# Query up-projection of the latent heads in five products, its weights split later, and the latent copies placed one by one

## The reference

```python
MLA_NOPE, MLA_ROPE, MLA_V = 64, 32, 64
MLA_Q_RANK, MLA_KV_RANK = 192, 128

def mla_q(zcq, g, w_uq, tabs):
    q = (rms_norm(zcq, g) @ w_uq).reshape(B, L, MLA_HEADS, MLA_NOPE + MLA_ROPE)
    q_nope, q_pe = jnp.split(q, [MLA_NOPE], axis=-1)
    if tabs is not None:
        q_pe = axial_rope(q_pe, tabs)
    return jnp.concatenate([q_nope, q_pe], axis=-1)

def mla_kv(zckv, zkr, g, w_ukv, tabs):
    kv = (rms_norm(zckv, g) @ w_ukv).reshape(B, L, MLA_HEADS, MLA_NOPE + MLA_V)
    k_nope, v = jnp.split(kv, [MLA_NOPE], axis=-1)
    ...
# per layer: adaLN -> one input projection -> o_a, o_b, o_m -> gates -> h @ w_out -> post-norm residual
o_m = block_attention(ql_m, jnp.concatenate([kc_m, kl_m], 1), jnp.concatenate([vc_m, vl_m], 1), MLA_SCALE)
```

## Time and profile before

| what | value |
|---|---|
| three runs | 953.35, 954.07, 954.11 us |
| profiled execution, its own time | 948.69 us |
| its span, first to last instruction | 946.6 us |
| busy: PE, DVE, POOL, ACT | 906.8, 560.1, 509.3, 429.5 us |
| mean granted clock of TensorE | 0.995 |
| instructions | 13414 |

### The profile page before, as it was taken

The page is one execution under the profiler, slowest core; times in us unless marked ns, Lnnn a source line. Parts: engine busy times, 40 slices in busy tenths (PEclk is TensorE's granted clock), DMA queues, the critical chain, the costliest instruction groups (busy, mean ns, idle before and its releaser), DMA issues.

```text
span 946.6 us, 13414 instructions
## 1 busy us (share of the span) xinstructions
PE 906.8 (96%) x4647; PEld 643.3 (68%) x4647; DVE 560.1 (59%) x903; ACT 429.5 (45%) x879; POOL 509.3 (54%) x433
## 2 busy tenths in 40 slices
PE   4999999999999999999999899999998999999996
PEld 3787767889745565665678789888984445555684
DVE  6569043513678679963318838567247758983347
ACT  5332121413566466655334853235335646655432
POOL 3246233324677645565547438455439876666572
PEclk9999999999999999999999999999999999999998
DMA  9968561314524200010343212323343221020252
GB/s 319 293 231 273 210 247 50 84 34 105 132 52 101 51 18 18 18 68 1 145 171 110 103 32 76 81 76 84 80 116 77 70 49 26 18 76 1 91 177 89
DMA packets 51753, 95.83 MB, mean 101 GB/s; under 512 B 9508, under 2 KB 24720, under 8 KB 50664
## 3 DMA queue, kind: packets, MB, share of 16 engines
q1 hardware_dynamic: 51688, 94.99, 33.1%
HBM read 71.32 MB, written 4.21 MB: 80 GB/s over the span
## 4 chain that ended last, share of the span: by engine, by line
PE 80%; DVE 7%; ACT 6%; POOL 2%; issue 2%; DMA 1%; SPq 1%; POOLq 0%; ACTq 0%; DVEq 0%
PE banks L998 14%; PE banks L1000 13%; PE banks L999 13%; PE banks L1293 13%; PE banks L1315 11%; PE banks L1238 4%; ACT area_z L1852 2%; PE banks L1009 2%; PE banks L1334 2%; PE banks L1267 1%; DVE negmax L2245 1%; PE banks L1327 1%; ACT late_bias L1829 1%; DMA w_raw<-in_w_in_dram 1%; DVE area_b L2422 1%
## 5 line engine op out<-in xcount | busy, mean ns | idle before, releaser
L1961 POOL TENSOR_TENSOR w_split<-w_raw,w_split 128x512 fp32r<-128x512 f32 (+4 forms) x122 | 146.8, 1212 | 216.2 <-ACT w_split L1570 216.2
L998 PE MATMUL banks<-w_split,area_a 128*128 128x512 f32 (+3 forms) x612 | 232.2, 379 | 6.3 <-POOL w_split L1961 3.2
L1000 PE MATMUL banks<-w_split,area_a 128*128 128x512 f32 (+3 forms) x612 | 224.9, 367 | 0.0
L999 PE MATMUL banks<-w_split,area_a 128*128 128x512 f32 (+3 forms) x612 | 224.3, 367 | 0.0
L2245 DVE TENSOR_REDUCE negmax<-banks 128x1 f32<-128x768 f32 x160 | 148.0, 951 | 79.7 <-PE banks L1238 55.9
L1570 ACT ACTIVATE w_split<-w_raw 128x512 fp32r<-128x512 f32 (+4 forms) x122 | 69.0, 580 | 195.8 <-PE banks L1000 183.5
L1688 ACT ACTIVATE area_z<-banks 128x512 f32<-128x512 f32 x196 | 108.2, 599 | 77.8 <-PE banks L1293 74.6
L998 PEld LDWEIGHTS banks<-w_split,area_a 128*128 128x128 f32 x612 | 115.5, 189 | 39.0 <-issue 19.1
L1293 PE MATMUL banks<-area_a 97*128 97x512 f32 (+4 forms) x448 | 127.8, 401 | 4.2 <-ACT area_z L1688 3.1
L1000 PEld LDWEIGHTS banks<-w_split,area_a 128*128 128x128 f32 x612 | 115.4, 188 | 16.5
L999 PEld LDWEIGHTS banks<-w_split,area_a 128*128 128x128 f32 x612 | 115.7, 189 | 12.8
(11 more groups left out here) (234 smaller groups left out, 1454.1 us busy)
## 6 DMA issues: line engine op xcount, KB each, us to landing
w_raw<-in_w_in_dram SPq DMA_DIRECT2D x32, 512.0 KB, 3.6
area_g<-in_w_ada_dram SPq DMA_DIRECT2D x13, 1024.0 KB, 5.3
area_g<-in_w_ada_dram SPq DMA_DIRECT2D x16, 512.0 KB, 5.5
w_raw<-in_w_out_dram SPq DMA_DIRECT2D x16, 512.0 KB, 4.8
area_a<-parts SPq DMA_DIRECT2D x72, 96.0 KB, 2.2
area_a<-parts SPq DMA_DIRECT2D x30, 192.0 KB, 3.6
area_b<-in_x_dram SPq DMA_DIRECT2D x8, 512.0 KB, 6.7
w_raw<-in_w_in_dram SPq DMA_DIRECT2D x8, 352.0 KB, 5.3
```

Source lines behind the costliest of these rows:

```text
L998: nc.tensor.matmul(dst, a[0], b[0], start=first, stop=False)
L999: nc.tensor.matmul(dst, a[0], b[1], start=False, stop=False)
L1000: return nc.tensor.matmul(dst, a[1], b[0], start=False, stop=last)
L1961: op = nc.gpsimd.tensor_tensor(lo, raw, hi.bitcast(F32), ALU.subtract)
```

## The change

The change has five parts, all in the attention or just ahead of it.

1. The rank of 192 is cut in 128 + 64 rows (`UQ = 128`). Of the second block the high part lies in rows 0 to 63 and the low part in rows 64 to 127 of the same tile; its weight slice of 64 rows is loaded twice, into rows 0 to 63 and 64 to 127 of its slot, with a second DMA. One product against the stacked block then does what two did, and a group of columns takes five products instead of six (three for block 0, two for block 1; the term low*low comes with them).
2. ACT: the copy of a unit's queries (`mla_high`) and that of its keys (`mla_high_keys`) are separate calls. The first unit's stand on either side of `exponent(p, 1)`, the second unit's on either side of `exponent(p, 3)`, where before both were ahead of `exponent(p, 2)`.
3. DVE: `mla_low` of both units stands behind `reduce_max(p+2, 1)`. Before, the first stood ahead of `reduce_max(p+1, 7)` and the second ahead of `reduce_max(p+2, 1)`.
4. PE: `max_tile` of a latent pair waits for the high parts instead of the low parts; the first score of the pair waits for the low parts of its second unit.
5. POOL splits slice 0 of `w_uq` in loop 0 and slice 1 in loop 3 (ACT's order of these stays). At the start of layer 0, POOL's split of the second slice of input weights waits until DVE has split the first rows of the normalized tokens (`h_ready`).

```diff
@@ constants, and the loading of the weights (SP) @@
-UQ = 96
+UQ = 128
...
                 elif kind == "uq":
-                    sp.dma_start(slot[0:UQ].rearrange("p a n -> p (a n)")[:, 0:576],
-                                 w_uq[L, a * UQ:(a + 1) * UQ, :]).then_inc(done, 16)
+                    flat = slot.rearrange("p a n -> p (a n)")[:, 0:576]
+                    if a == 0:
+                        sp.dma_start(flat, w_uq[L, 0:UQ, :]).then_inc(done, 16)
+                    else:
+                        rest = RANK_Q - UQ
+                        sp.dma_start(flat[0:rest], w_uq[L, UQ:RANK_Q, :]).then_inc(done, 16)
+                        sp.dma_start(flat[rest:2 * rest], w_uq[L, UQ:RANK_Q, :]).then_inc(done, 16)
...
@@ PE: mla_head, max_tile, scores @@
                     if what == "q":
-                        for j in range(2):
-                            mm = three(dst, [uq[:, i, j, h * P:(h + 1) * P] for i in range(2)],
-                                       [cmp_t[0:UQ, 2 * i + j, tokens(g)] for i in range(2)], j == 0, j == 1)
+                        w = [[uq[:, i, j, h * P:(h + 1) * P] for i in range(2)] for j in range(2)]
+                        three(dst, w[0], [cmp_t[:, 2 * i, tokens(g)] for i in range(2)], True, False)
+                        both = cmp_t[:, 1, tokens(g)]
+                        nc.tensor.matmul(dst, w[1][0], both, start=False, stop=False)
+                        mm = nc.tensor.matmul(dst, w[1][1], both, start=False, stop=True)
...
                     if family(u) == "mla":
-                        pe.wait_ge(mla_lo, N_MLA[L, u])
+                        pe.wait_ge(mla_hi, N_MLA[L, u])
...
                 if step == 0:
                     pe.wait_ge(mrow_in, 32 * (PN[L, p] + 1))
+                    if pair_family(p) == "mla":
+                        pe.wait_ge(mla_lo, N_MLA[L, 2 * p + 1])
@@ ACT: compressed_hi, mla_high, attend @@
-                r0, r1, hi = [(0, 96, 0), (0, 96, 1), (0, 128, 4), (64, 96, 6)][j]
+                r0, r1, hi = [(0, 128, 0), (0, 64, 1), (0, 128, 4), (64, 96, 6)][j]
...
-                f = operands(u)
-                copy(f[0][0:96, qcols(L)], qk_t[0:96, 2 * (m % 2), qcols(L)])
-                copy(f[2][0:64, :], qk_t[0:64, 2 * (m % 2) + 1, :]).then_inc(mla_hi, 1)
+                copy(operands(u)[0][0:96, qcols(L)], qk_t[0:96, 2 * (m % 2), qcols(L)])
+
+            def mla_high_keys(L, u):
+                m = N_MLA[L, u]
+                copy(operands(u)[2][0:64, :], qk_t[0:64, 2 * (m % 2) + 1, :]).then_inc(mla_hi, 1)
...
                     exponent(L, p, 1)
+                    if head_pair(p + 2):
+                        mla_high_keys(L, 2 * p + 4)
                     if context:
                         copy_context(L, p - 1)
                     else:
                         copy_latents(L, p - 1)
+                    exponent(L, p, 2)
+                    copy_denominators(L, p - 1)
                     if head_pair(p + 2):
                         mla_high(L, 2 * p + 5)
-                    exponent(L, p, 2)
-                    copy_denominators(L, p - 1)
                     exponent(L, p, 3)
                     copy_maxrow(L, p + 1)
+                    if head_pair(p + 2):
+                        mla_high_keys(L, 2 * p + 5)
                     if head_pair(p + 3):
                         mla_copy(L, 2 * p + 6)
@@ POOL @@
                     for s in chunks[0][:NW]:
+                        if s[3] == 1:
+                            pool.wait_ge(h_ready, N_H[0, 0, 0])
                         split_w(s)
...
-                    if p == 0:
-                        for j in range(2):
-                            split_w(("uq", L, j, 0))
+                    if p in (0, 3):
+                        split_w(("uq", L, int(p > 0), 0))
@@ DVE: compressed_lo, attend @@
-                    r0, r1, hi, lo = [(0, 96, 0, 2), (0, 96, 1, 3), (0, 128, 4, 5), (64, 96, 6, 7)][j]
+                    r0, r1, hi, lo = [(0, 128, 0, 2), (0, 64, 1, 1), (0, 128, 4, 5), (64, 96, 6, 7)][j]
+                    at = 64 if j == 1 else r0
...
-                    if head_pair(p + 2):
-                        mla_low(L, 2 * p + 4)
                     if not packed(p + 1):
                         reduce_max(L, p + 1, 7)
                     reduce_max(L, p + 1, 8)
...
-                    if head_pair(p + 2):
-                        mla_low(L, 2 * p + 5)
                     if not packed(p + 2):
                         reduce_max(L, p + 2, 1)
+                    if head_pair(p + 2):
+                        mla_low(L, 2 * p + 4)
+                        mla_low(L, 2 * p + 5)
                     if p == 2:
                         split_last(L)
                     reduce_max(L, p + 2, 2)
```

More of the change, by code:

```diff
@@ L291 @@
 for _n, _p in enumerate(PIECES):
-    _landed[_n % NRAW] += 16 * (len(CHUNKS[_p[2]]) if _p[0] == "in" else 1)
+    _landed[_n % NRAW] += 16 * (len(CHUNKS[_p[2]]) if _p[0] == "in" else 2 if _p[0] == "uq" and _p[2] else 1)
     RAW_VALUE[_p] = _landed[_n % NRAW]
@@ L496, in hybrid_layers @@
         ada_w = area_g[:].rearrange("p t d -> p (t d)").rearrange("p (s n) -> p s n", s=NADA)
-        uq = w_split[0:UQ].rearrange("p a b n -> p (a b n)").rearrange("p (s j n) -> p s j n", s=2, j=2)
+        uq = w_split[:].rearrange("p a b n -> p (a b n)").rearrange("p (s j n) -> p s j n", s=2, j=2)
         c_rows = scr[0:32, 1, 0:P]
@@ L965, in w_views @@
                 return [(src[:, z], hi[:, z], lo[:, z]) for z in range(2)]
-            src = flat[0:UQ, 0:576].rearrange("p (h n) -> p h n", h=6)
+            src = flat[:, 0:576].rearrange("p (h n) -> p h n", h=6)
             hi, lo = (uq[:, i, a, :].rearrange("p (h n) -> p h n", h=6) for i in range(2))
@@ L1141, in turn_compressed @@
                 _, L, j, g = use
-                a, b = [(0, 96), (96, 192), (192, 320), (256, 352)][j]
+                a, b = [(0, UQ), (UQ, RANK_Q), (192, 320), (256, 352)][j]
                 freed(pe, use)
@@ L2223, in compressed_lo @@
                     dve.wait_ge(hi_ready, N_HI[use])
-                    r0, r1, hi, lo = [(0, 96, 0, 2), (0, 96, 1, 3), (0, 128, 4, 5), (64, 96, 6, 7)][j]
-                    nc.vector.tensor_tensor(cmp_t[r0:r1, lo, tokens(g)], bank(use)[r0:r1, 0:len(GROUPS[g]) * P],
+                    r0, r1, hi, lo = [(0, 128, 0, 2), (0, 64, 1, 1), (0, 128, 4, 5), (64, 96, 6, 7)][j]
+                    at = 64 if j == 1 else r0
+                    nc.vector.tensor_tensor(cmp_t[at:at + r1 - r0, lo, tokens(g)], bank(use)[r0:r1, 0:len(GROUPS[g]) * P],
                                             cmp_t[r0:r1, hi, tokens(g)].bitcast(F32), ALU.subtract).then_inc(free_dve, 1)
```

## The result

The changed kernel takes 956.91 us, the median of six runs (956.46 to 958.39), against 953.7 us for the kernel before: a ratio of 1.0042, with a 95% interval of 1.0029 to 1.0056. It is slower, where 951.9 and faster was forecast.

The account below looks back on a forecast made before the run. PE, busy 96% of the span, was taken as the bound, with DVE near its limit in loops 5 and 6. Terms -1.2 + 0.1 + 0.2 - 1.1 - 0.2 = -2.2 us gave a 951.9 median, range 947.2 to 956.0.

Parts of the forecast that it names:

- Loop 7: Four subtractions ahead of reduce_max(9, 2) on DVE would cost 0 to +0.8 us a layer, +0.2 for both layers.
- Loops 5 and 6: One PE wait goes, another comes: +0.4 and -0.2 us in layer 0, +0.2 and -0.3 in layer 1, +0.1 together.
- The new wait: In loop 5, score (5,4)'s second product waits for ACT's copy to area_b, held by DVE's low part, until 357.6 to 359.6.
- The forecast's shift of 1.16: PE's first up-projection of loop 5 in layer 0 would come 1.16 us earlier, at 354.6 instead of 355.76.
- The 0.49: The maximum's wait of 0.49 us at 360.07 in loop 5 would go, since max_tile waits for the copy.
- The five products: 18 products fewer, 3.7 us; only pair 7's in loop 4 count separately, -1.2; the other 2.5 lie in loops 5 and 6.
- The late split: POOL's split of slice 1 moved to loop 3 removes a transfer wait in loop 1 of layer 1, -1.1 us.
- The second DMA of the slice: The extra load of 64 rows goes out among loads that land long before loop 4; no cost given.
- The start: POOL's second weight split waits for DVE's first rows, ready some 0.4 us earlier: -0.5 to +0.2, taken as -0.2.
- Rival C: Contended ends in loops 5 and 6 of both layers, two waits over 2 us bring half clock: +3.9, 958.0 us; chance 0.14.
- contended ends: High ends for loops 5 and 6, where subtractions take 1.92 to 2.04 us beside POOL: +3.0 over the four loops.
- The base: Profiled execution of the kernel before, 948.69 us, with the runs' median taken as 5.4 above it.

Follow-up runs that it names:

- e9: Changed kernel without POOL's wait at the start, first unit's copies and low part in their old places in loop 7 only: 952.1 us, ratio 0.9997.
- e10: Changed kernel without POOL's wait at the start, first unit's copies and low part in their old places in loops 5 and 6 only: 953.29 us, ratio 1.0011.
- e3: Changed kernel with the first unit's low part back in its old place on DVE, ACT's order as changed: 952.92 us, ratio 1.0008.
- e2: Changed kernel without POOL's wait for h_ready at the start: 955.41 us, ratio 1.0037.
- e12: e5 with PE's maxima waiting for the copies and a latent pair's first score for the low parts: 947.29 us, ratio 0.9943.
- e5: Kernel before with the five products and POOL's split of slice 1 in loop 3, old ACT and DVE orders: 947.85 us, ratio 0.9966.
- e4: Kernel before with the five products alone, all orders and waits as before: 949.6 us, ratio 0.9973.
- e6: Changed kernel without POOL's wait at the start, ACT's copies in the order before, DVE's low parts as changed: 963.2 us, ratio 1.0116.
- e11: Changed kernel with only the second unit's copies and low part moved, POOL's wait at the start kept: 947.59 us, ratio 0.995.
- e8: Changed kernel without POOL's wait at the start, only the second unit's copies and low part moved: 948.13 us, ratio 0.9957.

## Why the prediction was wrong

**Loop 7, the step that failed.** It was costed at "0 to +0.8 in a layer", +0.2 for both together, on the ground that "nothing of it shows where PE has products of its own for 2 us". Measured without a fall of the clock, loop 7 grew by 2.4 to 2.5 us in layer 0 (25.4, 25.5 against 23.0) and 1.7 in layer 1, +4.2 instead of +0.2. I had set the added work against PE's 2 us of products and had not asked when DVE gets to it: from 408.52 it works without a pause to 417.7, two of the four subtractions stand beside POOL's sums (2.06 and 2.02), and the reduction that PE wants is four subtractions, 5.7 us, behind the one before it. The forecast took such contended rows for loops 5 and 6 only. e9 shows the size (0.0040 of the time), e10 that the loss is there without loops 5 and 6, and e3, where only DVE's first low part went back, that DVE's row makes it: loop 7 is back at 23.0 and 19.7.

**Loops 5 and 6, right in mechanism.** The new wait is where the forecast put it, released by what it named. Up to loop 4 the changed kernel's profile runs 1.8 us behind the first one, by the fall of the clock at its start. Taken back by that, PE's second score product, forecast between 357.6 and 359.6, came at 358.7 (360.50 - 1.8), in the middle: one of the two subtractions was contended (2.03), the other hardly (1.07). The forecast's shift of 1.16 was more than its own terms give, 1.03 + 0.74 - 0.8 = 0.97; the first up-projection came at 356.57 - 1.8 = 354.8, where 354.6 was said. The loops as a whole (products included) changed by +0.2 and +0.1 in layer 0 and by +0.7 (e2, without a fall) and -0.4 in layer 1, +0.6 together, against +0.1. The 0.49 taken off because `max_tile` waits for the copy has no ground in that edit: in e12, which has it, the wait is 0.84, as it is 0.83 without it in e5.

**The five products, sized too small.** Loop 4 and its like in layer 1 gave 1.3 us, where 1.2 was said. But loops 5 and 6 gave 1.1 more (e4), though I had written that DVE near its limit makes a saved product worth little there. The time is 2.6 us lower by the ratio with the five products alone (1.2 to 4.0 by the interval), 3.1 by the medians.

**The late split, right**: -1.0 in loop 1 of layer 1 (forecast -1.1). That POOL works 55 to 60% of loop 3 was misread: in the kernel before it is busy for 13.47 of 19.22 us there in layer 0, 70%, and more in layer 1. No loss shows from the added split. **The second DMA of the slice**, costed at nothing, may not be: in every kernel with five products "between" is 0.5 to 1.2 us longer, and PE waits there for the transfer of ones_r, 0.4 to 1.1 us, where neither profile of before has such a wait. I did not run the doubled load by itself, so the cause stays open. **The start**: forecast -0.2, not measurable.

**The clock.** Rival C had the mechanism but asked for contended ends in all four loops and put two falls at the copy's waits, at 0.14. What came had one fall behind a wait of each kind, and the main loss from loop 7. By the runs' own records, (1 - clock) x span is 9.9 us for the changed kernel and 8.2 for the 26 runs of before, 5.0 for e5 and 12.2 for e6; what is left of the span is 945.3, 942.2, 941.4 and 948.7. So of the 4.8 us between the mean spans of the changed kernel and of those 26 runs, about 3.1 are waits less products and 1.7 are the clock; the records give the clock to 0.001, about 1 us. The Trainium skill ("TensorE: Matmul & The Clock Gate", section "HAM oscillation — how this bites in real kernels") tells of waits, longer ones than these, that are paid again in a cold clock; the trace agrees in some executions and not in others, as the pairs 1.68/1.69 and 1.96/1.88 show. The exclusive port of the Trainium skill ("SBUF — State Buffer", section "SBUF: two separate sides") fits all the rows of 2.02 to 2.06, which stand beside POOL's sums: the sentence in the forecast by which a row of four subtractions meets POOL again and again was the one to follow, for loop 7.

**The base.** The profile that the sum went by was of the quickest kind, 948.69; before's 39 runs of the first two comparisons go from 948.75 to 954.53. Adding its distance to the median was sound, but its start, with a clock of 1.00 throughout, is only one of two kinds: eight of the fourteen profiles, the second of before among them, have a fall there.

## What to carry to other kernels

When independent work on a shared engine is put in one row, cost the instruction behind the row by the row's whole length, at the contended durations, and for every consumer of the engine, in every loop where it happens and not only where the change was aimed. Orders on two engines that hand work to each other are to be moved together or not at all: here DVE's new order with ACT's old one cost 1.5% (e6 against e5), and ACT's new place of one copy with DVE's old order 0.6% (e3 against e11), while moving only the second of two units cost nothing. Before a difference of 2 us is explained, read the same stage in a second execution of the old kernel.

## What the runs showed of the hardware

- After a wait of PE of 1.7 to 2.1 us the clock fell in some executions and not in others of the same order of instructions: behind 2.08 in loop 5 of layer 1 it fell in the changed kernel and not in e2. A fall made a loop 1.5 us longer (23.3 against 21.8 there). It also fell behind a group of shorter waits, 0.79, 0.28 and 0.28 from 717 to 719 us: in the profiles of e5 and e8 the window from 720 to 725 us has a mean clock of 0.73, while in the kernel before, with the same three waits, it is 1.00.
- A product of 128x512 against the stacked block took as long as one of 96 rows: its starts are 357.37, 357.61 and, for the next product, 357.84 in the changed kernel, 0.23 us apart, and 356.10, 356.33 and 356.56 for 96 rows before.
- A subtraction on DVE with both operands in SBUF took 0.94 us alone and 2.02 to 2.06 beside POOL's sums; three reductions out of PSUM beside two such sums took 2.67 us, 0.9 each (408.57 in the kernel before, where POOL's sums run from 408.17 for 2.86 us), and one alone 0.95.
